# Sending the experts' outputs back to their tokens in five parts, with the turned one-hots made by a comparison

## The chip, the cores and the metric

The kernel runs on one core of one Trainium2 chip. Its time is the device time in microseconds (us), and the time before is the median of three runs. TensorE is called PE here, VectorE DVE, ScalarE ACT, GpSimd POOL; SP issues the large weight transfers. "Granted clock" is the share of TensorE's full 2.4 GHz that the chip granted.

## The reference, cut to what matters

The program is a transformer block (windowed attention with a bidirectional mLSTM, then experts that choose their tokens) followed by two further layers. The change lies in the expert stage of the first block and at the head of the first further layer. N is 512 tokens, D 1024, with 16 experts, 64 tokens for each:

```python
aff = softmax(h @ w_router)                        # 512 x 16
gate, idx = top_k(swapaxes(aff, 1, 2), 64)         # each expert takes 64 tokens
xg = h[bidx, idx]
g = einsum('becd,edf->becf', xg, w_gate); u = einsum('becd,edf->becf', xg, w_up)
y = einsum('becf,efd->becd', silu(g) * u, w_down) * gate[..., None]
x = x + g2 * zeros_like(h).at[bidx, idx].add(y)    # the way back
# next layer
h = rms_norm(x, attn_norm); proj = h @ w_in        # iq, ik, iw ("index rows") are 324 of its columns
```

## The kernel before, in words

Every engine has a function for each stage, and the order of its instructions is the order in which these functions are called; nothing is rescheduled. Events on semaphores tie the engines together. Weights stream from HBM in pieces of 512 KB, in an order fixed when the program is built, through a ring of 11 buffers (4 named RAW, 7 named RX, and XP for some early pieces). SP issues a piece's DMA (L3526) when the piece that last held its buffer has been used.

**The expert stage.** Two experts of 64 tokens make one group of 128 rows ("slots"), so there are eight groups. A one-hot matrix OH (tokens by slots) gathers the tokens: `pe_gather` (products at L2284) makes the gathered inputs XG for two groups at a time. `pe_moe` then runs `for s in range(9)`: `pe_gate_up(s)` (64 products, L2377, 16 weight pieces); for s of 1 to 3 the gather of the next two groups; `pe_slot_gates(s)` for s of 0 to 3, which sums the gates of the slots of two groups with products of OH and the affinities (L2335, two columns each, f32, recorded as two matmuls each); `pe_down(s - 1)` (32 products, L2417, 8 pieces); and `pe_act_turned(s)`, four transposes (L2388). ACT and DVE turn each group's result, times its gates, into a rounded half and a remainder (`act_out_of`, L2552, and L2622). These halves lie in OPH and OPL for groups 0 to 3, and in MY for 4 to 7.

**The way back** needs the one-hots turned (slots by tokens). At s of 4 and 5 `pe_onehot_turned` transposes OH, four transposes for a group (L2351), and ACT and DVE copy the results to OHT (L2362, L2364). `pe_back(part, ms)` then forms, for each 128 features m, the sum over the part's groups of (half of y) times OHT (L2433, 512 columns, two products for each group), and `dve_add` (L2084) adds it into the token matrix XT. There are three parts:

```python
BACK = ((0, 4), (4, 6), (6, 8))
back_at = {6: (0, range(0, 4)), 7: (0, range(4, 8)), 8: (1, range(8))}
```

so groups 0 to 3 go back half at s=6 and half at s=7, 4 and 5 at s=8 ahead of `pe_down(7)`, and 6 and 7 after it, as `pe_back(2, range(8), True)`. In this last part ACT makes the normalised operand (`act_gained`, L2098, into OPH) and the square of each m (L711), DVE the remainder (`dve_gained`, L2106, into OPL), and PE sums the squares over the partitions, one product of ones for each m (`pe_sum`, L703).

**The index rows.** `pe_rows2(0)` multiplies the normalised tokens by the 324 index columns: four pieces, each with two m (k = 0 and 1 for the first), four token tiles and three products (`mm3`, L643 to L645: high and low halves), so 24 products for a piece. A piece's high half is made by ACT (`act_hi`, L594) and its low half by POOL (`pool_lo`, L631), in three pairs of buffers, so the fourth piece's pair is that of the first. ACT makes three of them ahead of the last part's m=0, and the fourth after `act_root` (L715). PE sums the last square after the first piece and turns the row of root mean squares (`pe_root_rows`, L2229) after the second. DVE then takes its reciprocals (L2697, and L719 for the 512 of them), scales the index weights (L2786) and starts the rotary chain of the four token tiles (L822 to L856), on which ACT (L780 to L795) and POOL (L808) work too. `act_rows2` makes the high half of the third bq piece only after this chain's last root. On POOL a copy of a mask (L2816) stands between `pool_lo` of the third and the fourth index piece.

PSUM has eight banks, handed out in turn; a bank is used again when its reader is done.

Of the kernel before, what the change touches and what calls it, by code (L numbers as in the profile page):

```python
# [14 lines left out]
CST = {}  # L15

def constants():
# [29 lines left out]
    put("invf", np.tile(f(1) / p, (128, 1)))  # L48
    put("eps", np.full((128, 1), EPS, f))
    return np.concatenate(parts, 1).astype(f)  # L50

# [98 lines left out]
def body(nc, d, out, ctx):  # L150
# [11 lines left out]

    cst = sb("cst", [128, CONSTS.shape[1]])

# [50 lines left out]
    FF, FR = mem("FF", 6144, 3072), mem("FR", 9216, 20480, F32R)  # L215
    ORM = mem("ORM", 6144, 4096)

    def in_(t, o, n):
# [147 lines left out]
    s_vr, s_c, s_rb, s_bg, s_x, s_cx, s_out = (sem("s_" + n) for n in ("vr", "c", "rb", "bg", "x", "cx", "out"))  # L366
    s_cc, s_id = sem("s_cc"), sem("s_id")
    hi, lo_v, lo_p, zero_p = signal("hi"), signal("lo_v"), signal("lo_p"), signal("zero_p")
# [191 lines left out]
    def programs(T, V, A, G, Y):  # L560
# [329 lines left out]
        def act_setup():  # L890
            A.e.dma_start(crow[0:8], d["c"].rearrange("a (k p) -> (a k) p", p=128)).then_inc(s_cc, 16)
            A.e.dma_start(crow[8:16], d["c_ctx"].rearrange("(k p) -> k p", p=128)).then_inc(s_cc, 16)
            A.e.dma_start(cst[:, 0:256], d["cst"][:, 0:256]).then_inc(s_id, 16)
            A.wait_ge(s_cc, 32)
            set_a.up(A.e.activation(crow[0:16], crow[0:16], ACT.Silu), "cs")
            A.e.dma_start(cst[:, 256:], d["cst"][:, 256:]).then_inc(s_c, 16)
            for o, i in vload:
                A.e.dma_start(o, i).then_inc(s_vr, 16)
# [1341 lines left out]
        GC = in_(FM, 8464, 8)  # L2240
        A16 = [in_(FM, 512 * i, 512)[0:16, :] for i in range(2)]
# [6 lines left out]

        oht_copy = lambda g: "v" if g % 2 else "a"
# [77 lines left out]

        def pe_slot_gates(s):

            b = B.one()  # L2330
            B.clear(b)
            for j in range(2):
                g = 2 * s + j
                for q in range(4):
                    mm = T.e.matmul(ps(b)[:, 2 * j:2 * j + 2], OH[:, q, 128 * g:128 * g + 128].bitcast(F32),  # L2335
                                    AFF[:, q, 2 * g:2 * g + 2], start=(q == 0), stop=(q == 3))
            PB["gc", s] = b
            prod.up(mm, ("gc", s))
            B.give(b, (moe_v, ("gc", s)))

        def dve_slot_gates(s):
            V.wait_ge(*prod["gc", s])
            p2 = ps(PB["gc", s], 4).rearrange("p (g a) -> p g a", a=2)
            for i in range(2):
                moe_v.up(V.e.tensor_copy(GC[64 * i:64 * i + 64, 2 * s:2 * s + 2], p2[64 * i:64 * i + 64, :, i]), ("gc", s))

        def pe_onehot_turned(g):
            b = B.one()
            B.clear(b)
            for q in range(4):  # L2350
                mm = T.e.transpose(ps(b)[:, 128 * q:128 * q + 128], OH[:, q, 128 * g:128 * g + 128].bitcast(F32), ident)  # L2351
            PB["oht", g] = b
            turned.up(mm, ("oht", g))
            B.give(b, (copied, ("oht", g)))

        def copy_onehot(who, g):
            if oht_copy(g) != who:
                return
            E = V if who == "v" else A
            E.wait_ge(*turned["oht", g])  # L2360
            if who == "v":
                copy_v.up(V.e.tensor_copy(OHT[:, g, :], ps(PB["oht", g])), ("oht", g))  # L2362
            else:
                copy_a.up(A.e.activation(OHT[:, g, :], ps(PB["oht", g]), ACT.Copy), ("oht", g))  # L2364

# [56 lines left out]

        def pe_back(part, ms, stat=False):
            g0, g1 = BACK[part]
            for g in range(g0, g1):
                T.wait_ge(*copied["oht", g])
            for m in ms:
                b = B.one()
                B.clear(b)
                for g in range(g0, g1):  # L2430
                    T.wait_ge(*moe_v["y", g, m // 4])
                    for i, half in enumerate(ye(g, m // 4)):
                        mm = T.e.matmul(ps(b), half[:, 128 * (m % 4):128 * (m % 4) + 128], OHT[:, g, :],  # L2433
                                        start=(g == g0 and i == 0), stop=(g == g1 - 1 and i == 1))
# [3 lines left out]
                if stat and m:  # L2438
                    pe_sum("moe", m - 1, SQM, 512)

        def pe_moe():
# [42 lines left out]
            for s in range(9):  # L2484
# [5 lines left out]
                if s < 4:  # L2490
                    if s:
                        pe_gather_root(BEHIND[s])
                        for k in range(8):
                            pe_gather(k, BEHIND[s])
                    pe_slot_gates(s)
                elif s < 6:
                    for g in range(4 * s - 16, 4 * s - 12):
                        pe_onehot_turned(g)
                if s in back_at:
                    pe_back(*back_at[s])  # L2500
                if s:
                    pe_down(s - 1)
                if s < 8:
                    pe_act_turned(s)
            pe_back(2, range(8), True)

        def act_moe():
# [11 lines left out]
            for s in range(9):  # L2519
# [5 lines left out]
                if s < 4:  # L2525
                    if s:
                        act_gathered(BEHIND[s])
                elif s < 6:
                    for g in range(4 * s - 16, 4 * s - 12):
                        copy_onehot("a", g)  # L2530
                if s:
# [7 lines left out]
            for m in range(8):  # L2539
                A.wait_ge(*added[("moe", 2), m])  # L2540
                act_gained(("an", 0), m)
                act_square("moe", m, XT, SQM, 512)
            act_root("moe", 512, RST)

        def act_out_of(g):
            A.wait_ge(*moe_v["gc", g // 2])
            if g >= 4:

                A.wait_ge(*turned["oht", 7])
            for n in range(2):  # L2550
# [6 lines left out]
        def dve_moe():  # L2557
# [43 lines left out]
            for x in (2, 3):  # L2601
                for q in range(4):
                    onehot(x, q)
            for s in range(9):
                if s < 8:
# [3 lines left out]
                if s < 4:  # L2609
                    if s:  # L2610
                        dve_gathered(BEHIND[s])
                    dve_slot_gates(s)
                elif s < 6:
                    for g in range(4 * s - 16, 4 * s - 12):
                        copy_onehot("v", g)
                if s in back_at:
                    dve_back(*back_at[s])
                if s:
# [5 lines left out]
                if s < 8:  # L2624
                    copy_act("v", s)
            dve_back(2, range(8), ("an", 0))

        def dve_back(part, ms, nm=None):
            for m in ms:
                dve_add(("moe", part), m, lambda m: mod[:, 5, m, 0:1])  # L2630
                if nm and m:
                    dve_gained(nm, m - 1)
            if nm:
                dve_gained(nm, 7)

# [59 lines left out]
        def dve_rstd_rows(l):  # L2695
            V.wait_ge(*turned["rows", l])
            rstd.up(V.e.reciprocal(RSTR, ps(PB["rows", l], 4)), ("rows", l))  # L2697
            dve_rstd(summed_up(l), 512, RST)

        def pe_rows2(l):  # L2700
            lhs = lambda k, t: pair(HX1, k, 128 * t, 128 * t + 128)
# [801 lines left out]
        def sync_engine():  # L3503
            wide = False
            sync_tokens()
            for q in seq:
# [66 lines left out]
```

## Time and profile before

| what | value |
|---|---|
| median of the runs | 2382.99 us (2382.88 to 2383.8, 3 runs) |
| profiled execution, from first to last instruction | 2385.8 us |
| PE busy, share of that span | 2264.3 us, 95% |
| DVE busy | 1233.7 us, 52% |
| ACT busy | 852.7 us, 36% |
| POOL busy | 365.9 us, 15% |
| gate, up and down products of the experts | about 509.9 to 774.0 us |
| index rows | from 792.6 us |

The profiled execution is a run of its own. Its span is the only time shown of it, and it lies 2.8 us above the median of the others. PE's 95% is an average over the program. The expert stage differs: there the DMA engines are busy nearly without a break. In tables by stretch the DMA share of a saturated stretch reads 1.05.

### The profile page before, as it was taken

How to read it: one execution, taken by the hardware profiler on the slowest of the kernel's cores; microseconds unless marked ns; L12 is line 12 of the kernel's file. 1: busy time of each engine (PE TensorE's matmuls, PEld its weight loads, DVE VectorE, ACT ScalarE, POOL GpSimd, SP SyncE). 2: the span in 40 equal slices, each digit the busy share in tenths (PEclk: the TensorE clock that was granted, in tenths of full speed). 3: DMA queues.
4: the chain of work that ended last, by engine and by line, in shares of the span. 5: the costliest groups of instructions: out<-in, count | busy, mean ns of one | idle time of the engine just before them, and what ended most of it. 6: DMA issues, size and time to landing. Idle time of an engine off the chain costs nothing.

```text
span 2385.8 us, 28694 instructions
## 1 busy us (share of the span) xinstructions
PE 2264.3 (95%) x11081; PEld 1720.7 (72%) x11081; DVE 1233.7 (52%) x2315; ACT 852.7 (36%) x1498; POOL 365.9 (15%) x273
## 2 busy tenths in 40 slices
PE   7999998789879999999999999999999999999999
PEld 5875676655424776777878888887767788888887
DVE  5743446642112696666654424448776755543442
ACT  4434442422100445544342213334564434322231
POOL 0111023000000454432000000025543200000000
PEclk9999889989999999999999999999999999999999
DMA  8216210358999222221223332222212212333322
GB/s 300 59 51 236 89 36 11 125 190 319 365 387 328 80 80 62 63 80 54 80 89 105 97 97 89 93 89 71 87 55 72 71 62 80 106 102 95 96 87 80
DMA packets 198285, 281.48 MB, mean 118 GB/s; under 512 B 13278, under 2 KB 125448, under 8 KB 198152
## 3 DMA queue, kind: packets, MB, share of 16 engines
q1 hardware_dynamic: 197584, 278.47, 35.0%
q8 instruction: 89, 1.46, 0.2%
q10 hardware_dynamic: 568, 1.19, 0.1%
q14 instruction: 44, 0.36, 0.0%
HBM read 277.52 MB, written 2.10 MB: 117 GB/s over the span
## 4 chain that ended last, share of the span: by engine, by line
PE 79%; DVE 11%; DMA 4%; ACT 3%; issue 2%; SPq 1%; POOL 0%; DVEq 0%; ACTq 0%
PE PS L643 20%; PE PS L645 19%; PE PS L644 19%; PE PS L1417 3%; PE PS L2377 3%; PE PS L2417 2%; PE PS L1399 2%; DMA RX<-in_w_up_dram 1%; PE PS L2284 1%; DMA RAW<-in_w_up_dram 1%; DVE AL L846 1%; PE PS L2433 1%; PE PS L1409 1%; DVE AL L825 1%; DVE AL L838 1%
## 5 line engine op out<-in xcount | busy, mean ns | idle before, releaser
L643 PE MATMUL PS<-OPH,WHI 128*128 128x512 f32 x1224 | 499.5, 408 | 12.1 <-DVE AR L1254 5.0
L645 PE MATMUL PS<-OPH,WLO 128*128 128x512 f32 x1224 | 482.5, 394 | 0.0
L644 PE MATMUL PS<-OPL,WHI 128*128 128x512 f32 x1224 | 481.5, 393 | 0.0
L594 ACT ACTIVATE WHI<-RAW 128x1024 fp32r<-128x1024 f32 (+2 forms) x286 | 295.6, 1037 | 463.0 <-PE PS L645 454.9
L631 POOL TENSOR_TENSOR WLO<-RAW,WHI 128x1024 fp32r<-128x1024 f32 (+1 forms) x107 | 255.5, 2391 | 1331.6 <-ACT WHI L594 1328.2
L615 DVE TENSOR_TENSOR WLO<-RAW,WHI 128x1024 fp32r<-128x1024 f32 x179 | 214.6, 1201 | 370.3 <-ACT WHI L594 370.2
L643 PEld LDWEIGHTS PS<-OPH,WHI 128*128 128x128 f32 x1224 | 232.6, 190 | 78.9 <-issue 25.4
L645 PEld LDWEIGHTS PS<-OPH,WLO 128*128 128x128 f32 x1224 | 232.4, 190 | 50.6
L644 PEld LDWEIGHTS PS<-OPL,WHI 128*128 128x128 f32 x1224 | 233.0, 190 | 43.6 <-issue 1.0
L643 PE MATMUL PS<-WHI,OPH 128*128 128x512 f32 (+2 forms) x576 | 231.7, 402 | 11.5 <-POOL WLO L631 4.0
L645 PE MATMUL PS<-WHI,OPL 128*128 128x512 f32 (+2 forms) x576 | 218.6, 380 | 0.0
L644 PE MATMUL PS<-WLO,OPH 128*128 128x512 f32 (+2 forms) x576 | 217.8, 378 | 0.0
L643 PEld LDWEIGHTS PS<-WHI,OPH 128*128 128x128 f32 x576 | 109.2, 190 | 56.6 <-issue 32.3
L643 PE MATMUL PS<-FR,WHI 128*128 128x512 f32 x352 | 136.9, 389 | 0.0
L644 PE MATMUL PS<-FR,WHI 128*128 128x512 f32 x352 | 136.9, 389 | 0.0
L645 PE MATMUL PS<-FR,WLO 128*128 128x512 f32 x352 | 136.9, 389 | 0.0
L645 PEld LDWEIGHTS PS<-WHI,OPL 128*128 128x128 f32 x576 | 109.1, 189 | 20.2
L644 PEld LDWEIGHTS PS<-WLO,OPH 128*128 128x128 f32 x576 | 109.6, 190 | 16.2 <-issue 1.0
L3262 ACT ACTIVATE AL<-AL,AC 128x128 f32<-128x128 f32 (+3 forms) x128 | 71.0, 555 | 107.5 <-DVE AC L1423 107.0
L2377 PE MATMUL PS<-RX,FM 128*64 128x512 f32 x296 | 76.4, 598 | 15.4 <-DMA RX<-in_w_up_dram 9.0
L645 PEld LDWEIGHTS PS<-FR,WLO 128*128 128x128 f32 x352 | 66.1, 188 | 13.8
L643 PEld LDWEIGHTS PS<-FR,WHI 128*128 128x128 f32 x352 | 66.1, 188 | 13.8
(431 smaller groups left out, 3304.5 us busy)
## 6 DMA issues: line engine op xcount, KB each, us to landing
RAW<-in_w_in_dram SPq DMA_DIRECT2D x102, 512.0 KB, 3.6
RAW<-in_w_ffn_in_dram SPq DMA_DIRECT2D x88, 512.0 KB, 3.5
RX<-in_w_gate_dram SPq DMA_DIRECT2D x42, 512.0 KB, 7.2
RX<-in_w_down_dram SPq DMA_DIRECT2D x42, 512.0 KB, 11.4
RAW<-in_w_ffn_out_dram SPq DMA_DIRECT2D x40, 512.0 KB, 3.4
RAW<-in_w_mod_dram SPq DMA_DIRECT2D x36, 512.0 KB, 4.5
RX<-in_w_up_dram SPq DMA_DIRECT2D x32, 512.0 KB, 10.2
RAW<-in_w_up_dram SPq DMA_DIRECT2D x25, 512.0 KB, 9.2
```

The source lines that it names most:

```text
L594: hi.up(A.e.activation(q.fhi, q.flat, ACT.Copy), ("w", q.i))
L615: lo_v.up(V.e.tensor_tensor(q.flo, q.flat, q.fhi.bitcast(F32), ALU.subtract), ("w", q.i))
L631: lo_p.up(G.e.tensor_tensor(q.flo, q.flat, q.fhi.bitcast(F32), ALU.subtract), ("w", q.i))
L643: T.e.matmul(o, a[0], b[0], start=first, stop=False)
L644: T.e.matmul(o, a[0], b[1], start=False, stop=False)
L645: return T.e.matmul(o, a[1], b[0], start=False, stop=last)
L825: row_v.up(V.e.tensor_tensor(s3[:, h0:h1, :], q3[:, h0:h1, :], cs.unsqueeze(1).to_broadcast([128, h1 - h0, 64]), ALU.mult), (r, "cos"))
L1399: mm = T.e.matmul(PS[:, 512 * b + c0:512 * b + c0 + w], l_, r_, start=True, stop=True)
L1417: mm = T.e.matmul(u.o, u.pt[:, 128 * j:128 * j + 128], v_, start=(j == 0), stop=(j == nb - 1))
L2377: mm = T.e.matmul(PS[64 * i:64 * i + 64, 512 * b:512 * b + 512], XG[:, 2 * n + k, s0:s0 + 64], q.raw[:, k, :], start=(n == 0 and k == 0), ...
L2417: mm = T.e.matmul(PS[64 * i:64 * i + 64, o:o + 512], AE[:, g % 2, 2 * m + k, 64 * i:64 * i + 64], q.raw[:, k, :], start=(m == 0 and k == 0 ...
L3262: expd.up(A.e.activation(v.p, v.p, ACT.Exp, bias=v.nm, scale=-1.0, accum_out=v.rs), v.name)
```

## The change

The turned one-hots are no longer transposed on PE. `pe_slots` at s=0 sums, for all eight groups at once, the affinities (as a rounded half and a remainder) and the token's number, with six columns for each group, in the one-pass type; `dve_slots` takes the slots' token numbers OF and the gates GC from that. `dve_onehot_turned` compares a table of token numbers with OF. OHT holds four groups instead of eight. The table TOKENS is loaded by one more DMA on SP where the wide ring begins, ahead of the expert stage.

The way back has five parts: groups 0 and 1 at s=4, 2 and 3 at s=5, 4 and 5 at s=7, 6 at s=8, and 7 after `pe_down(7)`. The last part's m of 0 to 3 precede the index rows; 4 and 5 stand after the first piece of these, 6 and 7 after the second. The squares are added on DVE (L2120) and summed on PE in two products after the third piece; the row is turned after the fourth. On POOL the mask's copy moves behind the index and the first bq pieces.

```diff
@@
-        OHT = RT[:, :].rearrange("p (g n) -> p g n", g=8)
+        OHT = RT[:, 0:2048].rearrange("p (g n) -> p g n", g=4)
@@
-        BACK = ((0, 4), (4, 6), (6, 8))
-        back_at = {6: (0, range(0, 4)), 7: (0, range(4, 8)), 8: (1, range(8))}
+        BACK = ((0, 2), (2, 4), (4, 6), (6, 7), (7, 8))
+        part_of = {g: part for part, (g0, g1) in enumerate(BACK) for g in range(g0, g1)}
+        back_at = {4: 0, 5: 1, 7: 2, 8: 3}
+        turned_at = {3: (0, 1, 2, 3), 6: (4, 5), 7: (6, 7)}
@@
+        def pe_slots():
...
+            T.wait_ge(*moe_v["affinities"])
+            for g in range(8):
+                T.wait_ge(*moe_v["oh", g // 2, 3])
                 for q in range(4):
+                    mm = T.e.matmul(ps(b)[:, 6 * g:6 * g + 6], OH[:, q, 128 * g:128 * g + 128], AFX[:, q, g, :],
+                                    start=(q == 0), stop=(q == 3))
...
+        def dve_affinities():
+            A3 = AFF.rearrange("p t (g a) -> p t g a", a=2)
+            V.wait_ge(*moe_v.up(V.e.tensor_scalar(AFX[:, :, :, 0:2], A3, 1.0, None, ALU.mult)))
+            moe_v.up(V.e.tensor_tensor(AFX[:, :, :, 2:4], A3, AFX[:, :, :, 0:2].bitcast(F32), ALU.subtract))
+            moe_v.up(V.e.tensor_copy(AFX[:, :, :, 4:6], C("token").unsqueeze(2).unsqueeze(3).to_broadcast([128, 4, 8, 2])),
+                     "affinities")
+
+        def dve_slots():
...
+            V.wait_ge(*moe_v.up(V.e.tensor_copy(OF, p6[:, :, 4]), "of"))
             for i in range(2):
+                h = slice(64 * i, 64 * i + 64)
+                moe_v.up(V.e.tensor_copy(GC[h], p6[h, :, i]), ("high gates", i))
...
+        def dve_onehot_turned(g):
+
+            if g < 4:
+                V.wait_ge(s_tokens, 16)
+                V.wait_ge(*prod["xg", 7, 3])
             else:
+                V.wait_ge(*prod[("moe", part_of[g - 4]), 7])
+            moe_v.up(V.e.tensor_scalar(OHT[:, g % 4, :], TOKENS[:, :], OF[:, g:g + 1], None, ALU.is_equal), ("oht", g))
@@ pe_moe
-                    pe_slot_gates(s)
-                elif s < 6:
-                    for g in range(4 * s - 16, 4 * s - 12):
-                        pe_onehot_turned(g)
+                    else:
+                        pe_slots()
...
-            pe_back(2, range(8), True)
+            pe_back(4, range(0, 4))
+
+        def pe_moe_last(n):
+
+            if n < 2:
+                pe_back(4, range(4 + 2 * n, 6 + 2 * n))
+            elif n == 2:
+                pe_sum_added("moe", SQM)
+                pe_sum("moe", 7, SQM, 512)
+            else:
+                pe_root_rows(0)
@@ act_moe
             for m in range(8):
-                A.wait_ge(*added[("moe", 2), m])
+                A.wait_ge(*added[("moe", 4), m])
                 act_gained(("an", 0), m)
-                act_square("moe", m, XT, SQM, 512)
+                act_square_added("moe", m, SQM)
             act_root("moe", 512, RST)
@@ dve_moe
-            dve_back(2, range(8), ("an", 0))
+            for m in range(8):
+                if m >= 2:
+                    dve_square_added("moe", m - 1, SQM)
+                dve_add(("moe", 4), m, lambda m: mod[:, 5, m, 0:1])
+                if m:
+                    dve_gained(("an", 0), m - 1)
+            dve_gained(("an", 0), 7)
@@ pe_rows2
-                    lambda n: pe_sum(summed_up(l), 7, SQ5 if l else SQM, 512) if n == 0 else pe_root_rows(l) if n == 1 else None)
+                    pe_ffn_last if l else pe_moe_last)
@@ pool_rows2
-            idx_p.up(G.e.tensor_copy(mask_of(0), C("cmask", 384, 512)), ("mask", l, 0))
             for i in J["idx", l]:
                 pool_lo(i + 3)
+            idx_p.up(G.e.tensor_copy(mask_of(0), C("cmask", 384, 512)), ("mask", l, 0))
@@ sync_engine
+                    Y.e.dma_start(TOKENS[:, :], d["cst"][:, kept:]).then_inc(s_tokens, 16)
```

## Rows read from the trace of the kernel before

**Rows 1.** Expert stage by stretch: busy us by engine, PEclk, DMA share, GB/s.

```profile
640.00:660.00 20.00, 16.63 (x82) 6.37 (x80) 3.58 (x5) 3.06 (x5) 0.00 (x0) 1.00 1.05 387
...
552.00:554.00 2.00, 2.00 (x12) 0.60 (x10) 0.00 (x0) 0.00 (x0) 0.00 (x0) 1.00 0.00 0
...
586.00:588.00 2.00, 2.00 (x12) 0.58 (x10) 0.00 (x0) 0.00 (x0) 0.00 (x0) 1.00 0.27 96
...
716.00:718.00 2.00, 2.00 (x11) 1.65 (x10) 0.78 (x2) 0.00 (x0) 0.00 (x0) 1.00 1.05 385
```

**Rows 2.** The chain that ended last, 565 to 775: start, length, what.

```profile
575.66 7.68 PE PS L2284 x64
...
583.34 1.68 PE PS L2335 x16
...
585.02 7.02 PE PS L2417 x32
...
646.86 1.90 PE PS L2351 x16
...
732.69 9.94 DMA RAW<-in_w_up_dram
...
759.78 7.29 PE PS L2433 x32
```

**Rows 3.** DVE's additions into XT, all of L2084: min/median/max ns.

```profile
L2084 DVE SCALAR_TENSOR_TENSOR XT<-PS,MOD,XT x40: 741/751/752, 351.7 to 791.8; 128x512 f32<-128x512 f32 x40
```

**Rows 4.** ACT's normalised operand by line, 700 to 1160: count, busy, mean ns.

```profile
L2098 ACT ACTIVATE OPH<-XT,VT 128x512 fp32r<-128x512 f32 x8 | 5.8, 721 | 7.4 <-DVE XT L2084 7.4
```

**Rows 5.** Around the last part: start, length, engine, line, idle before it.

```profile
774.01 2.11 PE L2433 MATMUL PS<-RT,MY 128*128 128x512 f32 x8
...
774.72 2.00 ACT L594 ACTIVATE WHI<-RAW 128x648 fp32r<-128x648 f32 x3
...
775.54 3.10 POOL L631 TENSOR_TENSOR WLO<-RAW,WHI 128x648 fp32r<-128x648 f32 x2 [352.91 <-ACT WHI L594]
...
777.37 1.82 DVE L2106 SCALAR_TENSOR_TENSOR OPL<-XT,VT,OPH 128x512 fp32r<-128x512 f32 x1 [0.45 <-ACT OPH L2098]
...
778.00 1.84 PE L703 MATMUL PS<-FM,cst 128*128 128x512 f32 x2 [1.88 <-ACT FM L711]
...
778.37 0.62 ACT L711 ACTIVATE FM<-XT 128x512 f32<-128x512 f32 x1
...
792.59 0.71 PE L643 MATMUL PS<-WHI,OPH 128*128 128x324 f32 x1
...
796.55 1.02 PE L703 MATMUL PS<-FM,cst 128*128 128x512 f32 x2
...
799.01 1.58 POOL L631 TENSOR_TENSOR WLO<-RAW,WHI 128x648 fp32r<-128x648 f32 x1 [18.15 <-ACT WHI L594]
```

**Rows 6.** DVE adding squares elsewhere, all of L2120: min/median/max ns.

```profile
L2120 DVE TENSOR_TENSOR AR<-AR x6: 684/691/693, 450.3 to 467.9; 128x512 f32<-128x512 f32 x6
```

**Rows 7.** The granted clock behind PE's pause, columns as in rows 1.

```profile
780.00:781.00 1.00, 1.00 (x4) 0.74 (x3) 0.00 (x0) 0.00 (x0) 0.86 (x1) 0.50 0.79 166
...
782.00:783.00 1.00, 1.00 (x5) 0.68 (x4) 0.99 (x2) 0.63 (x2) 0.00 (x0) 1.00 0.85 221
```

**Rows 8.** Start of the rotary chain, columns as in rows 5.

```profile
801.60 3.32 DVE L719 RECIPROCAL RST<-RST 128x512 f32<-128x512 f32 x1
...
806.17 0.22 DVE L2786 TENSOR_SCALAR AL<-PS,SM 128x4 f32<-128x4 f32 x1 [1.24 <-PE PS L645]
...
807.58 1.56 DVE L825 TENSOR_TENSOR AL<-AL,RC 128x256 f32<-128x256 f32 x1
...
817.92 2.00 ACT L594 ACTIVATE WHI<-RAW 128x1024 fp32r<-128x1024 f32 x2
...
819.04 7.33 POOL L631 TENSOR_TENSOR WLO<-RAW,WHI 128x1024 fp32r<-128x1024 f32 x3 [0.34 <-ACT WHI L594]
...
821.56 0.47 PE L643 MATMUL PS<-WHI,OPH 128*128 128x512 f32 x1 [1.18 <-POOL WLO L631]
```

More of the change, by code:

```diff
@@ L49, in constants @@
     put("eps", np.full((128, 1), EPS, f))
+    put("token", i[:, None] + 128.0 * np.arange(4)[None])
+    put("tokens", np.tile(np.arange(512, dtype=np.float32), (128, 1)))
     return np.concatenate(parts, 1).astype(f)
@@ L161, in ps @@
         return PS[0:m, 512 * b:512 * b + n]
-    cst = sb("cst", [128, CONSTS.shape[1]])
+    kept = CST["tokens"][0]
+    cst = sb("cst", [128, kept])
     def C(name, a=0, b=None, p=128, p0=0):
@@ L216, in body @@
     ORM = mem("ORM", 6144, 4096)
+    TOKENS = mem("TOKENS", 30208, 512)
     def in_(t, o, n):
@@ L2341, in dve_slot_gates @@
-        def dve_slot_gates(s):
-            V.wait_ge(*prod["gc", s])
-            p2 = ps(PB["gc", s], 4).rearrange("p (g a) -> p g a", a=2)
-            for i in range(2):
[L2345 to L2354, printed above, removed]
@@ new lines, in pe_slots @@
+            PB["slots"] = b
+            prod.up(mm, "slots")
+            B.give(b, (moe_v, "slots"))
+        def dve_affinities():
[4 more added lines that the diff above has]
+                     "affinities")
@@ new lines, in dve_slots @@
+        def dve_slots():
+            V.wait_ge(*prod["slots"])
+            p6 = ps(PB["slots"], 48).rearrange("p (g a) -> p g a", a=6)
+            V.wait_ge(*moe_v.up(V.e.tensor_copy(OF, p6[:, :, 4]), "of"))
+            for i in range(2):
+                h = slice(64 * i, 64 * i + 64)
+                moe_v.up(V.e.tensor_copy(GC[h], p6[h, :, i]), ("high gates", i))
+            V.wait_ge(*moe_v["high gates", 1])
+            for i in range(2):
+                h = slice(64 * i, 64 * i + 64)
+                moe_v.up(V.e.tensor_tensor(GC[h], GC[h], p6[h, :, 2 + i], ALU.add), *(["slots"] if i else []))
@@ L2421, in pe_down, with pe_back @@
                 B.give(b + n, (moe_v, ("y", g, n)))
-        def pe_back(part, ms, stat=False):
+        def pe_back(part, ms):
             g0, g1 = BACK[part]
             for g in range(g0, g1):
-                T.wait_ge(*copied["oht", g])
+                T.wait_ge(*moe_v["oht", g])
             for m in ms:
@@ L2432, in pe_back @@
                     for i, half in enumerate(ye(g, m // 4)):
-                        mm = T.e.matmul(ps(b), half[:, 128 * (m % 4):128 * (m % 4) + 128], OHT[:, g, :],
+                        mm = T.e.matmul(ps(b), half[:, 128 * (m % 4):128 * (m % 4) + 128], OHT[:, g % 4, :],
                                         start=(g == g0 and i == 0), stop=(g == g1 - 1 and i == 1))
@@ L2539, in act_moe @@
             for m in range(8):
-                A.wait_ge(*added[("moe", 2), m])
+                A.wait_ge(*added[("moe", 4), m])
                 act_gained(("an", 0), m)
-                act_square("moe", m, XT, SQM, 512)
+                act_square_added("moe", m, SQM)
             act_root("moe", 512, RST)
         def act_out_of(g):
-            A.wait_ge(*moe_v["gc", g // 2])
+            A.wait_ge(*moe_v["slots"])
             if g >= 4:
-                A.wait_ge(*turned["oht", 7])
+                A.wait_ge(*prod["xg", 7, 3])
             for n in range(2):
@@ L2611, in dve_moe @@
                         dve_gathered(BEHIND[s])
[L2612 to L2615, printed above, removed]
+                    else:
+                        dve_slots()
+                for g in turned_at.get(s, ()):
+                    dve_onehot_turned(g)
                 if s in back_at:
-                    dve_back(*back_at[s])
+                    dve_back(back_at[s])
                 if s:
@@ L2625, in dve_moe, with dve_back @@
                     copy_act("v", s)
-            dve_back(2, range(8), ("an", 0))
-        def dve_back(part, ms, nm=None):
-            for m in ms:
+            for m in range(8):
[5 more added lines that the diff above has]
+            dve_gained(("an", 0), 7)
+        def dve_back(part):
+            for m in range(8):
                 dve_add(("moe", part), m, lambda m: mod[:, 5, m, 0:1])
[L2631 to L2634, printed above, removed]
         HEADS_BEST = [("head", i, h) for i in (1, 2, 3) for h in range(4)]
@@ L2698, in dve_rstd_rows, with pe_ffn_last @@
             dve_rstd(summed_up(l), 512, RST)
+        def pe_ffn_last(n):
+            if n == 0:
+                pe_sum(summed_up(1), 7, SQ5, 512)
+            elif n == 1:
+                pe_root_rows(1)
         def pe_rows2(l):
```

32 lines of the change are left out of this document (6 added, 26 removed).

## The prediction

> **What bounds the kernel now.** The page's shares say PE, at 95%. But in the expert stage PE waits for weights, so I read that stage by stretches first. From 640 to 660 us PE is busy for 16.63 of 20 us while the DMA engines move 387 GB/s, their ceiling here, and DVE is busy for only 3.58 us [rows 1]. The stage runs at the weights' pace wherever the DMA share reads 1.05. That rate fails where SP has no free buffer. At 552 to 554 it is 0 and at 586 to 588 96 GB/s, each time while or just after PE has spent a long stretch without using a piece: two gather products' sets and the slot gates [rows 1, 2]. The reader should then follow the chain of waits. It goes through a weight transfer (732.69 to 742.6), and behind it PE works alone: two sets of columns back, two sets of down products, and the last set of columns [rows 2]. Last come the timeline of the last part and the start of the rotary chain [rows 5, 8]. There PE, ACT and DVE hand each m to one another, and the index rows start only at 792.59, 18.6 us after the last part's first product at 774.01. I call that product's time D and count the tail from it.
>
> **1. Columns back.** A part of two groups is 32 products in 7.29 us, 0.228 each [rows 2]. Before, 96 of them stand behind the last gate/up piece (half of part 0, part 1, part 2). After, 64 do: groups 4 and 5, then 6, then 7. Of the 32 saved, 16 precede D: 16 x 0.228 = 3.7 us earlier. The other 16 lie in the last part, which I count with the tail. The 64 products now at s=4 and s=5 fall where PE waits: there two weight sets of 24 pieces need 24 x 524 KB / 387 GB/s = 32.5 us each, and PE's own work is 64 products of 0.217 (13.9), 7.0 down, 0.6 turned and 7.3 back, or 28.8 us. Does the 7.3 us stretch dry the ring? A stretch of that length (the first half of part 0) runs around 716 in the trace, and at 716 to 718 the rate is 385 GB/s [rows 1]. So nothing is paid. If that cover were gone, it would be up to 7.3 us for each of the two.
>
> **2. Slots and turned one-hots.** The slot gates go: 1.68 us at each of s=1, 2, 3 [rows 2] and the same at s=0. The transposes go too, 1.90 us at each of s=4 and 5 [rows 2], but PE waits for weights there, so that is worth nothing. New at s=0 are 32 one-pass products of six columns. The trace has none. The nearest are the gates' own, 16 recorded matmuls in 1.68 us, 0.105 each, and I take that: 3.4 us. Bounds: half of it (1.7, nothing in the rows excludes a shorter one) and the two records of an old product (6.7). Up to the end of the s=1 gather PE is thus 3.4 - 1.7 - 1.7 = 0, nothing gained. At s=2 and s=3 the stretch between pieces falls from 1.1 + 7.7 + 1.7 = 10.5 to 8.8 us. The ring ran dry around 586, 11.5 us after the stretch began at 574.5, and DMA needs about 3 us behind the stretch's end (585.0) to be back at speed. 10.5 + 3 - 11.5 = 2 us dry before, 8.8 + 3 - 11.5 = 0.3 after. That is 1.7 us of transfer time at each of two steps, 3.4 us, handed on to the last piece. Bounds: 0 (the dry stretch has another cause) and 5.1 (slots at 1.7).
>
> DVE gets 16 more additions of 0.751 [rows 3] (12.0 us), eight comparisons of at most 0.75 each instead of four copies, and some small operations. Its 3.6 busy us in 20 [rows 1] hide them. The one place where they queue is s=8: eight additions of part 3 (5.6 us) stand before y(7) on DVE, but PE needs 3.7 + 7.0 us for part 3 and the down products. ACT loses four copies, hidden before. TOKENS is 256 KB on SP's queue ahead of the stage, 0.7 us at 387 GB/s, ahead of pieces that then sit unused for tens of us: 0 (at most 0.7).
>
> **3. The tail, from D** (all on the old clock, D = 774.0). ACT is busy with three index halves for 2.00 us from 774.72 [rows 5], as before, then makes m=0, m=1 and both squares, until 779.0. Now DVE adds the squares ahead of each further addition. POOL's third low half is no longer behind the mask's copy and runs from about 778.6 to 780.2. Beside POOL the remainder at 777.37 took 1.82 us [rows 5], against 0.75 for the addition of the same shape [rows 3], so I let the first square sum end at 780.6. m=2 is added by 781.3, and the remainder of m=1, which the first index piece needs, is ready at 782.0. **The first piece starts at 782.1** instead of 792.6.
 With the first 3.8 us at half clock the piece takes 5.3. It ends at 787.4. Product m=4, DVE's addition and the remainder of m=3 (0.6 + 0.75 + 0.7) put the second piece at 789.5 to 793.05, and the same for m=6 the third at 795.15 to 798.7. DVE and ACT keep that pace: 0.67 + 0.72 + 0.62 + 0.69 = 2.7 us for each m [rows 3 to 6]. Two sums (0.9 + 1.0) end at 800.6.
> **What is late next:** ACT makes the fourth piece's high half only after `act_root`: 0.7 + 0.75, then POOL 1.58 [rows 5]. The fourth piece runs from 803.7 to 807.3. Only then is the row turned, and DVE's 3.32 us reciprocal [rows 8] comes behind it, uncovered: the rotary chain starts at 811.2, against 806.17 [rows 8]. That is **5.0 us later from D**, though PE itself is 1 us ahead. Behind this chain ACT makes the third bq piece's high half (817.92), POOL its low half (819.04, 2.39), and PE had already waited 1.18 us for it at 821.56 [rows 8]; so the chain's delay passes to PE in full. Corrections: POOL's low halves no longer meet the first tile, whose 256-column product took 1.56 us, where 512 columns take 0.69 [rows 6, 8]: -0.9. The 3.1 us pause before the fourth piece may lower the clock again, 0 to +1.8: I take +0.9. Bounds of the tail: +1 (no low clock, all waits overlapped) and +14 (below).
>
> **Sum**, on the profiled execution's span: 2385.8 - 3.7 - 3.4 + 5.0 - 0.9 + 0.9 = 2383.7 us. The median of the runs lies 2.8 below that span, so 2382.99 - 2.1 = **2380.9 us**.
>
> **Rivals.** *The tail keeps its lead* (28%). The rotary chain starts no later than before from D, since the first piece runs at full clock (-1.75, and the steps behind it follow), the squares' sum finds POOL idle (-1) and the chain's slack on DVE absorbs the rest. Then all 7.1 us count: 2375.9 us. For it: PE is 10 us earlier at the first piece. Against: the order of ACT's queue and the reciprocal, which nothing covers.
> *The weights do not come earlier* (16%). The dry stretches stay, or the slots cost 6.7 and dry the ring once more. Then -3.7 + 5.0 = +1.3: 2384.3 us. For it: the ring also went dry at s=1, where XP buffers are not refilled. Against: the 385 GB/s beside a 7.3 us stretch.
> *Slower: the index rows run at the low clock* (12%). PE computes in bursts of 3.6 us with waits of 1 to 3 us between. If the clock does not come back in them, the four pieces take 24 x 0.27 = 6.5 us each: +1.2 and three times +2.9, or +10 over my tail: 2390.9 us. It turns the sign from +2.1, less than one further piece at 1.2 GHz. For it: one pause of 1.88 us was enough to lose it [rows 5, 7]. Against: from 782 on it read 1.00, though PE then waited for each m.
> (The Trainium skill, TensorE: Matmul & The Clock Gate, in its section on HAM oscillation, says that a kernel whose products wait between bursts can keep falling to half clock. By that rule the time would be this rival's; the trace agrees only with the first fall.)
> *My forecast* has 44%. Its own range is 2378.5 to 2384, from 1.8 us of clock, 1.7 us in the slots and 1 us in the tail.
>
> **Chances.** A measurement of this kernel can tell about 0.2%, 4.8 us, from no change. Below 2378.2: the first rival and a little of the forecast, 0.32. Above 2387.8: the last rival and a share of the third, 0.13. Within: 0.55. The range of 8 in 10 runs from 2374.5, past the first rival, to 2387.5, past the second.
>
> **What would show it.** Right: the first L2377 waits unchanged, DMA share 1.05 through 584 to 590; the last gate/up piece about 3.4 us earlier and D about 7 us; no dry stretch at s=4 and 5; the first index piece 8 us after D; a PE wait of about 3 us for POOL before the fourth; L719 after it; the third bq piece 5 us later from D than 47.6. Wrong: a dry ring at s=4, a chain that starts within 33 us of D, or PEclk at 0.50 through all index rows.

## The result and the profile after

The changed kernel is a little slower: 2388.86 us (median of 20 runs) beside 2381.73 us for the kernel before, ratio 1.0032 [1.0021, 1.0044]. The forecast was 2380.9 us, with 2387.5 us as the upper end of its range. One of the 20 runs took 4901.73 us and is left out of the ratio.

The profiled span is 2387.7 us, 1.9 above that of before. I aligned PE's instructions of the two traces one by one. The table shows how far the changed kernel is ahead (-) or behind (+) at each place.

| place | offset, us | gained or lost since |
|---|---|---|
| ahead of the expert stage (510) | -4.0 | chance: PE's program is the same up to there, and in the other runs this offset lies between +0.6 and -13.0 |
| D, first product of the last part | -9.7 | -5.7 |
| end of the query and key rows (890) | -4.0 | +5.7 |
| 900, first further layer | -1.0 | +3.0 |
| 1684, second further layer | -1.6 | -0.6 |
| 1700 | +1.4 | +3.0 |
| end | +1.7 | +0.3 |

Offsets are rounded, so sums can be 0.1 off. The gain to D and the loss in the tail cancel. What is left are two equal losses of 3.0 us, in a place that the prediction never looked at. From 510 to the end the changed kernel loses 5.7 us, which fits the ratio (its interval is 5 to 10.5 us).

**The expert stage.** By stretches of the changed kernel (us, then busy us of PE, PEld, DVE, ACT, POOL, then PEclk, DMA share, GB/s):

```profile
640.00:660.00 20.00, 20.00 (x92) 10.19 (x92) 8.20 (x11) 1.86 (x3) 0.00 (x0) 1.00 1.04 382
...
548.00:550.00 2.00, 2.00 (x12) 0.72 (x10) 0.00 (x0) 0.00 (x0) 0.00 (x0) 1.00 0.00 0
...
582.00:584.00 2.00, 2.00 (x12) 0.62 (x10) 0.00 (x0) 0.69 (x1) 0.00 (x0) 1.00 0.86 270
```

and from its chain that ended last:

```profile
519.85 3.67 PE PS L2342 x32
...
572.02 7.66 PE PS L2290 x64
579.68 7.02 PE PS L2428 x32
...
640.37 7.52 PE PS L2444 x32
...
673.01 7.49 PE PS L2444 x32
...
753.72 3.66 PE PS L2444 x16
```

The 32 six-column products took 3.67 us (forecast 3.4). Between gather (L2290) and down products (L2428) no gates stand any more. At s=1 the ring still runs dry, as before (0.00 at 548); at s=2 the worst two microseconds move 270 GB/s, where it was 96 [rows 1]. At s=3 a dip stays: 124 GB/s from 616 to 618, where the kernel before fell to 66 GB/s from 622 to 624. The columns back at s=4 and s=5 (7.5 us each, L2444) dry nothing. Ahead of D stand 16 products fewer, 3.66 us.

**The tail.** Timeline of the changed kernel from D, which is 764.35 here (start, length, engine, line; in brackets the idle time before it and who ended that):

```profile
764.35 2.11 PE L2444 MATMUL PS<-RT,MY 128*128 128x512 f32 x8
...
769.42 2.04 DVE L2124 TENSOR_TENSOR FM<-FM 128x512 f32<-128x512 f32 x1
769.65 0.39 PE L647 MATMUL PS<-WHI,OPH 128*128 128x324 f32 x1 [3.19 <-DVE OPL L2110]
...
772.93 0.61 PE L647 MATMUL PS<-WHI,OPH 128*128 128x324 f32 x1 [2.60 <-ACT OPH L2102]
...
780.45 0.39 PE L647 MATMUL PS<-WHI,OPH 128*128 128x324 f32 x1 [0.68 <-ACT OPH L2102]
...
785.92 0.39 PE L647 MATMUL PS<-WHI,OPH 128*128 128x324 f32 x1 [0.75 <-ACT OPH L2102]
...
794.08 0.39 PE L647 MATMUL PS<-WHI,OPH 128*128 128x324 f32 x1 [3.10 <-ACT WHI L598]
...
799.34 0.40 PE L2233 MATMUL PS<-cst,RST 1*128 1x1 f32 x4
799.88 3.32 DVE L723 RECIPROCAL RST<-RST 128x512 f32<-128x512 f32 x1
803.12 0.12 DVE L2809 TENSOR_SCALAR AL<-PS,SM 128x4 f32<-128x4 f32 x1
```

Read it beside [rows 5, 8]. The index rows start 5.3 us after D instead of 18.6. Yet DVE scales the first index weights (L2809) 38.8 us after D instead of 32.2. Between stand PE's pause of 3.1 us for the fourth piece and the uncovered reciprocal. The profile puts the pause down to ACT, but the piece's high half was done at 792.3. POOL made the low half right behind it:

```profile
792.42 6.22 POOL L635 TENSOR_TENSOR WLO<-RAW,WHI 128x648 fp32r<-128x648 f32 x3 [21.50 <-ACT WHI L598]
```

The first of these three ended at 794.0, and PE started at 794.08: it waited for POOL, and POOL for ACT's late high half. The granted clock fell three times, to half (1.2 GHz), each time behind pauses of PE (3.19 and 2.60 us, 3.10 us, and 3.40 us ahead of the third bq piece). One row of the first fall, one after it, and one of each later fall:

```profile
775.00:776.00 1.00, 1.00 (x5) 1.00 (x5) 0.52 (x1) 1.00 (x2) 0.00 (x0) 0.50 0.02 6
778.00:779.00 1.00, 1.00 (x7) 0.86 (x6) 0.11 (x1) 0.00 (x0) 0.00 (x0) 1.00 0.00 0
795.00:796.00 1.00, 1.00 (x5) 1.00 (x5) 0.00 (x0) 0.00 (x0) 1.00 (x1) 0.50 0.86 150
819.00:820.00 1.00, 1.00 (x4) 0.81 (x3) 1.00 (x3) 0.00 (x0) 1.00 (x2) 0.50 0.94 356
```

**The new waits.** At the head of the sparse query rows PE waited 0.71 us for a turned tile's copy before. Kernel before:

```profile
895.39 0.47 PE L643 MATMUL PS<-WHI,OPH 128*128 128x512 f32 x1 [0.71 <-DVE AL L883]
```

Changed kernel, first and second further layer, and the clock behind the first:

```profile
893.04 0.47 PE L647 MATMUL PS<-WHI,OPH 128*128 128x512 f32 x1 [2.73 <-DVE AL L2828]
...
1688.77 0.60 PE L647 MATMUL PS<-WHI,OPH 128*128 128x512 f32 x1 [2.73 <-DVE AL L2828]
```

```profile
894.00:895.00 1.00, 1.00 (x4) 0.50 0.46 51
896.00:897.00 1.00, 1.00 (x4) 0.50 0.56 215
```

L2828 is DVE's copy of the first tile of value rows (`bv`) out of PSUM. PE waits for it because the first tile of the query rows (`aq`) is to go into the same bank. `B.one()` hands out the eight banks in turn, and the change alters how many are asked for: one for the slots instead of four, none for the turned one-hots instead of eight, 40 for the columns back instead of 24. The counts alone do not give the shift, since `one()` passes over banks that are still held and `two()` takes an aligned pair. As the program allocates them, the ring stands one bank further back when the further layer begins. The four tiles of `bq` had banks 5, 6, 7, 0 before and have 4, 5, 6, 7 after. `aq`'s first tile takes bank 4 in both. The last reader of that bank was the copy of the last `bk` tile, long done, and is now that of the first `bv` tile, a moment ago.

### The profile page after: what moved, and what is told of

The parts are those of the page before. It is cut to its first block, busy times and chain, and to the rows that moved or that the text cites. A ratio compares the mean times of both kernels' runs of the same rounds, so it can differ in the third digit from the quotient of the medians.

```text
span 2387.7 us, 28572 instructions
## 1 busy us (share of the span) xinstructions
PE 2249.8 (94%) x11005; PEld 1711.6 (72%) x11005; DVE 1249.7 (52%) x2341; ACT 849.8 (36%) x1494; POOL 365.4 (15%) x273
## 3 DMA queue, kind: packets, MB, share of 16 engines
q1 hardware_dynamic: 197728, 278.73, 35.8%
## 4 chain that ended last, share of the span: by engine, by line
PE 78%; DVE 11%; DMA 4%; ACT 3%; issue 2%; SPq 1%; POOL 0%; DVEq 0%; ACTq 0%
PE PS L647 20%; PE PS L649 19%; PE PS L648 19%; PE PS L1421 3%; PE PS L2388 3%; PE PS L2428 2%; PE PS L1403 2%; DMA RX<-in_w_up_dram 1%; PE PS L2290 1%; DVE AL L850 1%; PE PS L2444 1%; PE PS L1413 1%; DVE AL L829 1%; DVE AL L842 1%; DMA RAW<-in_w_up_dram 1%
## 5 line engine op out<-in xcount | busy, mean ns | idle before, releaser
L635 POOL TENSOR_TENSOR WLO<-RAW,WHI 128x1024 fp32r<-128x1024 f32 (+1 forms) x107 | 255.6, 2394 | 1327.3 <-ACT WHI L598 1325.7
```

Of the source, the lines that this page charges most:

```text
L635: lo_p.up(G.e.tensor_tensor(q.flo, q.flat, q.fhi.bitcast(F32), ALU.subtract), ("w", q.i))
```

## Experiments

All experiments were timed in five rounds beside the kernel before, on one chip for each group of four. The diffs are shortened to the lines that matter. "Tail" is the offset gained or lost from D to 890 against the profile of before, "DVE" the time from D to the first scaled index weight (32.2 before, 38.8 after).

| kernel | ratio to before | 510 to D | tail | DVE, D + |
|---|---|---|---|---|
| the change | 1.0032 [1.0021, 1.0044] | -5.7 | +5.7 | 38.8 |
| e1_bank | 1.0009 [0.9995, 1.0024] | -4.9 | +5.3 | 38.1 |
| e2_before_shift (of the kernel before) | 1.0039 [1.0024, 1.0054] | -0.3 | -0.3 | 31.8 |
| e3_old_tail | 0.9982 [0.9968, 0.9997] | -4.6 | -2.5 | 29.7 |
| e4_cover | 0.9994 [0.9979, 1.001] | -3.8 | +4.1 | 32.1 |
| f1_gate_late | 0.9983 [0.997, 0.9997] | -5.9 | -0.7 | 31.7 |
| g1_gate_only | 1.0002 [0.9987, 1.0017] | -5.8 | +2.8 | 35.8 |
| g2_half_only | 0.9989 [0.9972, 1.0005] | -5.7 | +2.5 | 34.7 |
| f4_fill | 0.9998 [0.9982, 1.0013] | -4.3 | +3.3 | 36.7 |
| f3_pe_sums | 0.9987 [0.9969, 1.0004] | -6.1 | +1.2 | 33.3 |
| f2_slots_in_four | 0.9969 [0.9952, 0.9986] | -6.6 | -1.7 | 30.5 |
| g3_all_mended | 0.999 [0.9972, 1.0007] | -7.5 | -0.4 | 32.2 |
| g4_f2_again | 0.9972 [0.9955, 0.9989] | -6.1 | -1.2 | 31.0 |

**The banks.** e1_bank turns the ring back by one ahead of the index rows; e2_before_shift turns it by one in the kernel before.

```diff
 def pe_rows2(l):                    # e1_bank, on the change
+    if l == 0: B.i += 1             # ahead of pe_rows(("idx", l), ...)
 def pe_rows2(l):                    # e2_before_shift, on the kernel before
+    if l == 0: B.i += 7             # ahead of index_ = index(l, "pe")
```

> The kernel after, with one PSUM bank skipped ahead of the index rows, so that bq, bk, bv and aq get the banks that they have in the kernel before. Theory B (the banks): the change hands out another number of banks and so turns the ring by one, in both further layers; the first aq tile then waits for DVE's copy of bv (2.73 us in the profile after, 0.71 before), and each such pause lets the granted clock fall for 3.4 us. Undone, it gives back 2 x (2.0 + up to 1.7) = 4 to 7 us: 0.998 to 1.001 of before, against 1.0032 for the change. Theory C (the tail's chain: the rotary chain starts 6.6 us later from the last part): nothing changes, 1.003. Theory W (weights and columns moved): nothing changes either, 1.003. Banks right: no wait of the first aq tile on the bv copy, in either layer.

> The kernel before, with the PSUM ring turned by one bank ahead of bq of the first further layer, and nothing else: bv and aq then share a bank as in the kernel after. Theory B: the same pause in both layers, + 4 to 7 us, 1.0015 to 1.003 of before. Theories C and W: 1.000.

e1_bank's waits at that product are those of before:

```profile
892.18 0.47 PE L647 MATMUL PS<-WHI,OPH 128*128 128x512 f32 x1 [0.66 <-DVE AL L887]
...
1685.24 0.47 PE L647 MATMUL PS<-WHI,OPH 128*128 128x512 f32 x1 [0.69 <-DVE AL L887]
```

and e2_before_shift, which has nothing of the change, has the long ones and the low clock behind them:

```profile
894.64 0.47 PE L643 MATMUL PS<-WHI,OPH 128*128 128x512 f32 x1 [2.73 <-DVE AL L2807]
...
1690.75 0.47 PE L643 MATMUL PS<-WHI,OPH 128*128 128x512 f32 x1 [2.73 <-DVE AL L2807]
```

```profile
896.00:897.00 1.00, 1.00 (x4) 0.50 0.65 84
```

Its offset rises by 3.1 and 3.0 us at the two places, and it takes 1.0039 [1.0024, 1.0054] of the time before. So one bank costs 6 us in the trace of either kernel, shown from both sides. By the ratios it is 5.5 us on the change and 9.3 us on the kernel before (more than the 4 to 7 us expected, but the interval begins at 5.7). With the ring as before, the change costs nothing that can be measured; it gains nothing either.

**The old tail.** e3_old_tail keeps five parts and the slots, and puts the last part's order back: eight columns, a sum by PE behind each, then the index rows.

```diff
-            pe_back(4, range(0, 4))
+            B.i += 4                           # bq's banks as before
+            pe_back(4, range(0, 8), True)      # True: pe_sum behind each m
-    pe_back(4, range(4 + 2 * n, ...)), pe_sum_added(...)   # amid the index rows
+    pe_sum("moe", 7, SQM, 512) if n == 0 else pe_root_rows(0)
```

> The kernel after with the end of the kernel before: the last part's eight m ahead of the index rows with a sum of squares for each, the last sum after the first index piece, the row turned after the second, and the ring set so that bq gets its old banks. The five parts, the slots and the compared one-hots stay. What the expert stage gains (5.8 us up to the last part in the profiles, and half of the last part's products) is kept, and nothing is lost behind it: Theories B and C: 6 to 8 us under before, 0.9965 to 0.9975. Theory W (the moved columns and their transfers are what costs): above before, 1.002 or more.

It is faster than both kernels. Its ratio is above the 0.9965 to 0.9975 expected, with an interval that reaches down into them. Its index rows start 16.1 us after D, and the reciprocal lies beside them:

```profile
782.22 0.72 PE L647 MATMUL PS<-WHI,OPH 128*128 128x324 f32 x1
...
790.70 0.41 PE L2233 MATMUL PS<-cst,RST 1*128 1x1 f32 x4
...
795.78 0.22 DVE L2805 TENSOR_SCALAR AL<-PS,SM 128x4 f32<-128x4 f32 x1 [1.21 <-PE PS L649]
```

With D at 766.08 the root row is turned at D + 24.6, in the changed kernel at D + 35.0. What of the change is left behind D here (above all the last part of a single group) is worth 2.5 us. The index products amid its columns, together with the squares added on DVE, cost 7.8 (+5.3 in e1_bank against -2.5).

**Which wait of the tail.** e4_cover and f1_gate_late take away both the late high half and the reciprocal; g1 and g2 only one each. All have e1's banks.

```diff
 for m in range(8):                     # act_moe: e4, f1, g2, g3, f3
     act_square_added("moe", m, SQM)
+    if m == 5: act_hi(J["idx", 0][0] + 4)
 def dve_rstd_rows(l):                  # e4, f1, g1, g3, f3
-    dve_rstd(summed_up(l), 512, RST)
+    if l: dve_rstd(summed_up(l), 512, RST)
+    dve_rstd(summed_up(0), 512, RST)   # e4: behind dve_rope_end(first + 3);
+                                       # f1, g1, f3: at the end of dve_rows2
```

> The kernel after with the bank skipped, the fourth index piece's high half made by ACT after m=5 instead of after the root, and DVE's reciprocal of the 512 root mean squares moved behind the rotary chain of the index rows. Theory C: the wait for POOL before the fourth piece (3.4 us) and the uncovered 3.3 us go, and the pauses' low clock with them: the rotary chain starts 32 us after the last part's first product instead of 38.8, and the time is 5 to 8 us under e1_bank: 0.995 to 0.998 of before. Without Theory C (the chain's delay is made good further on) it is as e1_bank within 0.1%.

> e1_bank with two waits of the tail taken away: the high half of the fourth index piece is made by ACT ahead of the last three columns (e4 had that), and the 3.3 us reciprocal of the 128x512 row goes behind all of DVE's work on the query, key and value rows of this layer, so that it can no longer stand ahead of the turned copies where e4 gave its gain back (4.2 us). Theory C (what the new tail loses against the old one is this wait and this reciprocal, with the low clock that the wait brings): the rotary chain starts about 5 us earlier after the last part's first product than in e1, 4.5 to 5.2 us stay to the end, time 0.9985 to 0.9990 of before against 1.0009 for e1. Rival (the reciprocal costs the same wherever it stands, since DVE is late there too): 1.5 us or less stays, 1.0003.

> e1_bank with the 3.3 us reciprocal of the 128x512 row alone moved behind DVE's work on the query, key and value rows; ACT still makes the fourth index piece's high half after the root. Splits f1's gain of 4.5 us (6.6 us in the tail's chain). If the two waits stand one behind the other on the chain, each gives its own length: DVE starts on the index rows 3.3 us earlier after the first product of the last part than in e1, and PE gives back the 1.9 us for which it waited in f1 where the reciprocal now stands, so about 1.5 us less than e1 in the end (1.0003 of before). Rival: the rotary work waits for PE's late fourth piece anyway and the reciprocal was covered; then nothing at the tail, and 1.9 us more than e1.

> e1_bank with ACT's high half of the fourth index piece alone made ahead of the last columns, the reciprocal at its old place. The pause of PE ahead of the fourth piece (3.1 us) and the low clock behind it go: the four root products start 3.3 us earlier after the first product of the last part than in e1 (31.0 for 34.3 us), and as much stays to the end, 0.9995 of before. Rival: PE then waits for POOL's low half in place of ACT's high half, and 1 us or less is left.

In e1_bank, DVE reaches the index weights at D + 38.1. Without the reciprocal it is D + 35.8 (-2.3), with the early high half D + 34.7 (-3.4), with both D + 31.7 (-6.4). The two stand one behind the other, as g1 and g2 expected, though the reciprocal gave 2.3 for 3.3: the step itself is 3 us shorter in g1, but the row was turned 0.7 us later, for which I have no cause. The rivals of g1 and g2 (covered; POOL instead) are out. Where the reciprocal goes matters as much. In e4_cover it stood ahead of the turned copies, and PE waited there:

```profile
810.09 3.34 DVE L723 RECIPROCAL RST<-RST 128x512 f32<-128x512 f32 x1
...
814.37 1.29 PE L872 MATMUL PS<-cst,AL 128*128 128x128 f32 x4 [4.17 <-DVE AL L887]
```

so of the 6.0 us that the chain gained only 1.2 are left at 890, and e4_cover missed the 0.995 to 0.998 expected. Behind the value rows (f1, g1) the reciprocal still costs a wait of 1.6 us and 2.1 us of offset from 890 to 900. In g1 that is most of the 2.5 us that its tail had gained, so f1's rival (the reciprocal costs nearly the same wherever it stands) holds for this place. This is PE from 885 to 900 in f1_gate_late (total, times, longest):

```profile
PE PS L1403 <- DVE AC L1427: 1.6, 1, 1.6
```

**The clock's share.** f4_fill puts products that nobody reads into the three pauses of e1_bank's tail.

```diff
+def pe_fill(n):                        # 5, 3 and 5 of them
+    for _ in range(n):
+        T.e.matmul(ps(b), C("ones"), cst[:, 0:512], start=True, stop=True)
```

> e1_bank with thirteen products whose result nobody reads in PE's pauses of the tail: five ahead of the first index piece (pause of 3.2 us), three before its second half (2.1 us), five before the fourth piece (3.1 us), each 0.51 us at full clock. If the low clock behind these pauses (0.50 for some 3.4 us from 771 and again from 794 in e1) is a cost of its own, it goes: 1.7 us at each place, 3.4 us less, 0.9995 of before. Rival (the pieces' own waits set the tail and the low clock hides beside them, or the fillers run over the pauses): same as e1 or up to 1 us slower.

The clock stayed at 1.00 where e1_bank had 0.50. First f4_fill, 8 and 30 us after its D (757.37), then e1_bank 30 us after its own (765.52):

```profile
765.00:766.00 1.00, 1.00 (x4) 0.49 (x3) 0.82 (x2) 0.80 (x2) 0.00 (x0) 1.00 0.92 274
...
787.00:788.00 1.00, 1.00 (x9) 1.00 (x8) 0.00 (x0) 0.00 (x0) 1.00 (x2) 1.00 0.86 260
```

```profile
795.00:796.00 1.00, 1.00 (x5) 1.00 (x5) 0.00 (x0) 0.00 (x0) 1.00 (x1) 0.50 0.41 45
```

The tail is 2.0 us shorter in the profile, not 3.4. Some of the low clock may have hidden beside waits for columns; no run separates that. The two intervals of the ratio overlap, so the size rests on the traces alone.

**DVE's pace.** f3_pe_sums is f1 with PE summing each column's squares again.

```diff
-    act_square_added("moe", m, SQM)     # and DVE's dve_square_added
+    act_square("moe", m, XT, SQM, 512)  # and pe_sum behind each product
```

> f1_gate_late with the squares of the last part summed by PE per column (eight products by the ones, as in before) in place of DVE's additions; the index pieces still stand amid the columns. Theory P (DVE's pace of 2.74 us a column, against some 1.9 in the old tail, sets when the last column and the root are done): columns end 5 us earlier, and the tail is 2 to 4 us shorter than f1's though PE has six more products of 0.51 us; 0.9975 of before. Rival (PE or the index pieces' loads set it): the six products add up to 3 us, 0.9990 to 1.0003.

The ratio's interval holds both forecasts; the trace decides for the rival. The tail grew by 1.9 us instead of shrinking. PE now waits 5.1 us for ACT's squares (four waits, from 764 to 800):

```profile
PE PS L707 <- ACT FM L715: 5.1, 4, 2.8
```

Its clock also fell once more, at 895, where f1's did not: it loses 3.1 us from 890 to 900, f1 2.1.

**The slots.** In e1, e3, e4 and f4 the clock fell behind the 32 short products; row of e1_bank (its 510 to D is 0.8 us poorer than the change's):

```profile
525.00:526.00 1.00, 1.00 (x4) 0.27 (x4) 0.00 (x0) 0.04 (x1) 0.00 (x0) 0.50 1.04 385
```

f2_slots_in_four is e3_old_tail with eight short products at each of s=0 to 3, and the bank counter left alone to keep bq's banks.

```diff
-def pe_slots():
-    for g in range(8):
+def pe_slots(s):                        # and dve_slots(s), at s = 0 to 3
+    for g in (2 * s, 2 * s + 1):
```

> e3_old_tail with the slots' 32 six-column products dealt over s=0 to 3, eight each behind each stage's gate and up products, as the kernel before dealt its gates; DVE's five small operations go with them. Theory K (a run of 3.7 us of six-column products in one piece is what lowers the granted clock at 525, which three of the four kernels that have it showed): no stretch at 0.50 between 520 and 530, some 1.8 us less ahead of s=1, 0.9974 of before where e3 was 0.9982. Rival (the low clock there is chance, or the time of the slots is just spread): the same time as e3 within 0.5 us, or slower by the DVE operations that are added, about 1 us. The banks of the query pieces are as in before and e3.

It has the lowest ratio, 0.9969. Of the nine profiles with the long run, four lost the clock there and gained 3.8 to 4.9 us from 510 to D; the other five gained 5.7 to 6.1. The three with the split run lost it never and gained 6.1 to 7.5. So a fall behind the long run is possible, not certain; on average the split gained 0.9 us over the runs without a fall (6.7 for 5.8) and 2.3 over those with one (4.4). Whether f2 beats e3 isn't shown: they ran in different groups and their intervals overlap.

**All mended.** g3_all_mended is f1 with the slots split (and the ring set again for the same banks) and the reciprocal where DVE waits 3.1 us for ACT; g4_f2_again is f2's file, on the same chip.

```diff
 def dve_rope(r):                        # g3_all_mended
+    if r == rope_no[("idx", 0), 0] + 13: dve_rstd(summed_up(0), 512, RST)
     V.wait_ge(*row_a[r, "s"])
```

> The changed kernel with everything mended that the runs named: banks as in before, the fourth piece's high half early, the slots' products dealt over s=0 to 3, and the 3.3 us reciprocal at a place where DVE waits 3.1 us for ACT (ahead of the sum over a row tile of the sparse queries, at about 918) . If the causes are complete: as f1 without its 1.9 us of waiting at 893, so some 2 us below f1, 0.9970 of before, level with the old tail of g4. Rival: DVE's reciprocal meets a wait of PE there too, and the time is f1's (0.998).

> f2_slots_in_four once more, beside g3 on one chip: the old tail against the mended new one. Expected 0.997 of before again; if the interleaved index products are worth anything once their waits are mended, g3 is below it by 1 us or more, if not, it is level or above.

g3's profile is in line with the sum of its mends: nothing lost between 890 and 900, tail -0.4. Its ratio, 0.999 [0.9972, 1.0007], is above the 0.9970 that I expected, which lies just outside its interval; it holds the rival's 0.998, and g4's interval overlaps it. The interleaved index rows, mended, are level with the old tail at best.

One loss came in by the way. f2 and g4 both lose 4 us near 930, which e3 and g3 do not. First DVE and PE in f2_slots_in_four:

```profile
928.43 2.74 DVE L829 TENSOR_TENSOR AL<-AL 128x512 f32<-128x512 f32 x1
...
931.79 0.41 PE L1413 MATMUL PS<-cst,AL 128*128 128x128 f32 x2 [4.03 <-DVE AC L1427]
```

then DVE in e3_old_tail:

```profile
931.56 0.69 DVE L829 TENSOR_TENSOR AL<-AL 128x512 f32<-128x512 f32 x1
```

POOL makes a low half (L635) beside it, from 928.28 in f2 and from 931.77 in e3. So in e3, and likewise in g3, DVE's rotary product starts 0.2 us ahead of POOL and takes 0.69 us. In f2 and g4 it starts just behind POOL and takes 2.7, PE's wait grows from 1.6 to 4.0 us, and the clock reads 0.50 behind it: 2.4 us of waiting and 1.6 more. This is read from four traces; no run was made to test it.

## Why the prediction was wrong

**The step that failed** is the sum. It ended at the third bq piece and took everything behind it as unchanged. The change hands out another number of PSUM banks, and that moved a wait of 2.73 us, with a stretch at 1.2 GHz behind it, into both further layers: +6.0 us against a forecast of 0. Without it (e1_bank, 1.0009, 2383.57 us) the time is inside the forecast's range, but not at its centre: 2380.9 us is 0.9991 of before, below e1's interval. In the trace the forecast was -2.1 us from 510 to the end and +5.7 came: 6.0 from the banks, 1.4 from step 2, 0.7 from the tail, and -0.3 elsewhere. The kernel's text said that the banks are handed out in turn, so this could have been worked out blind.

**Step 1, columns back:** right. 16 products took 3.66 us (3.7), and 7.5 us of columns at s=4 and 5 dried nothing.

**Step 2, slots:** the price of the products was right (3.67 for 3.4). The gain was mis-sized: 3.4 us were forecast, 1.7 each at s=2 and 3, and 2.0 came in all (5.7 - 3.7). The dry stretch went at s=2 alone; at s=3 the dip to 124 GB/s stayed. By the chain that ended last, the last pieces of the gate/up sets came 0.3 us later at s=1 (forecast 0), then 1.1, 2.5 and, at the last set, 2.0 us earlier. To D this makes -5.7 for -7.1.

**Step 3, the tail:** right in mechanism and nearly in size. The first piece was expected at D + 8.1 to 13.4. Its first three products ran at D + 5.3 and the rest from D + 8.6 to 13.9, at the low clock. The fourth was forecast at D + 29.7 behind a pause of 3.1; it came at D + 29.7 behind 3.10. As forecast, that wait ended with POOL's low half. DVE's chain was forecast 5.0 later than before and came 6.6 later; the fourth piece ran at the low clock and took 5.3 us instead of 3.6, which the sum had booked apart, at +0.9. The third bq piece was forecast at D + 52.6:

```profile
817.27 0.47 PE PS L647
```

which is D + 52.9. That it is this near is partly luck: the chain began 1.6 us later than forecast and won 1.3 back on the way, 0.9 of it in the first tile's product (0.66 us instead of 1.56, as the sum had booked apart). The net tail was +5.7 for +5.0; g1 and g2 show that the late high half and the uncovered reciprocal, both named in advance, are its causes.

**Rivals.** The tail kept no lead, the weights did come earlier in part, and the clock came back between the pieces (1.00 at 778). The rival "slower" had the sign, but its mechanism was absent; slower came from elsewhere. The chance of 0.13 for slower was too low because every case that I priced lay between 510 and 822 us.

(The Trainium skill, TensorE: Matmul & The Clock Gate, in its section on HAM oscillation, says that waits between bursts of products let the clock fall. The pauses of 2.73 and 3.10 us here each had a stretch at half clock behind them. It was one stretch each time, not a lasting oscillation.)

## What to carry to other kernels

Where buffers or banks are handed out in turn, an edit that asks for one more or one fewer moves every later user of the ring. Compare the assignment before and after, and look for the first user whose predecessor is now a recent one. And starting work earlier gains nothing if its last piece still waits for the end of the same chain: here 13 us of head start at the first index piece ended as a loss of 6.6 us at the chain, since a half made late and a reciprocal lost their cover.

## What the runs showed of the hardware

- A pause of PE of 2.73 us in place of 0.7 cost 3.0 to 3.1 us at each of four places (the change and e2_before_shift). The wait grew by 2.0 us, but the products ahead of it were done 0.4 us sooner, so the product behind it started 1.6 us later, and 1.4 us more went in the stretch at half clock that followed.
- A run of 32 products of six columns, PE busy throughout, was followed by a granted clock of 0.50 in four of nine profiles, and none of three profiles with runs of eight had one there.
- In f4_fill, products by ones (f32, 128x512, 0.51 us each), one after another in PE's pauses, kept the clock at 1.00 through the tail.
- A DVE product of two 128x512 inputs took 0.69 us when it started ahead of POOL's low half (e3, g3) and 2.72 to 2.74 us when it started just behind it (f2, g4).
